# Layer 0's input projection loaded by rows in four pieces instead of by column slices, and its latent part accumulated piece by piece

## The reference, cut to what matters

```python
def conv_mla_mixer(x, cos, sin, w_in, b_in, conv_w, conv_b, ...):
    h = x @ w_in + b_in                      # (256, 1024) @ (1024, 1440)
    conv_in = h[..., :1024]                  # value | gate of the convolution, 4 chunks of 128 channels each
    q_lat, kv_lat, k_rope = h[..., 1024:1280], h[..., 1280:1408], h[..., 1408:]   # "latent" part, 416 columns
    ...
    u = a * jax.nn.sigmoid(g)                # then depthwise conv of width 31 (conv_w: 31 x 512)
    q  = rms_norm(q_lat, q_norm_g) @ w_uq
    kv = rms_norm(kv_lat, kv_norm_g) @ w_ukv
    o = causal_block_attention(q, k, v, ...)
    return jnp.concatenate([u, o], axis=-1) @ w_out + b_out
```

## Time and profile before

| | |
|---|---|
| device time, median of 3 runs | 1470.88 us (1467.9 to 1471.5) |
| span of the profiled execution, first to last instruction | 1469.8 us |
| time of the profiled execution beside its span | not listed apart from the span |
| PE busy | 1402.9 us, 95% of the span |
| DVE, ACT, POOL busy | 38%, 26%, 5% |
| DMA | 447.33 MB, mean 304 GB/s |
| chain that ended last | PE 90%, DVE 4%, issue 3%, ACT 1%, DMA 1% |

### The profile page before, as it was taken

One profiled execution on the slowest core, in us unless ns is written; L12 is line 12 of the kernel. 1 busy time (PEld: TensorE's weight loads), 2 busy tenths in 40 slices (PEclk: granted clock), 3 DMA queues, 4 the chain that ended last, 5 costly groups with the idle time before them and its releaser, 6 DMA issues.

```text
span 1469.8 us, 19916 instructions
## 1 busy us (share of the span) xinstructions
PE 1402.9 (95%) x7220; PEld 727.8 (50%) x7220; DVE 564.8 (38%) x1147; ACT 388.1 (26%) x857; POOL 76.7 (5%) x100
## 2 busy tenths in 40 slices
PE   6988999999999999999699999999999999999996
PEld 4764744444444444444288857444444444444441
DVE  2593534333333333433422235333333333333324
ACT  2561222222222222222122222222222222222221
POOL 2251100000000000000140000000000000000000
PEclk9999999999999999999899999999999999999998
DMA  9223679989999999998831415699889999999980
GB/s 338 83 115 143 235 286 381 379 346 378 381 382 381 381 379 381 380 377 345 278 137 58 163 38 230 279 381 381 358 361 382 380 380 383 380 382 380 381 360 30
DMA packets 80326, 447.33 MB, mean 304 GB/s; under 512 B 7437, under 2 KB 25289, under 8 KB 30616
## 3 DMA queue, kind: packets, MB, share of 16 engines
q1 hardware_dynamic: 77264, 439.25, 74.1%
q0 software_dynamic: 1904, 6.46, 1.3%
q10 hardware_dynamic: 1112, 1.01, 0.2%
HBM read 445.61 MB, written 1.05 MB: 304 GB/s over the span
## 4 chain that ended last, share of the span: by engine, by line
PE 90%; DVE 4%; issue 3%; ACT 1%; DMA 1%; DVEq 0%; POOLq 0%; POOL 0%; SPq 0%; ACTq 0%
PE bank L910 30%; PE bank L932 16%; PE bank L884 12%; PE bank L978 10%; PE bank L769 4%; PE bank L733 4%; PE bank L646 2%; PE bank L772 2%; PE bank L920 2%; PE bank L837 2%; DVE mixT L1635 2%; DMA ring<-in_l_w_in 1%; PE bank L947 1%; PE bank L875 1%; PE bank L628 1%
## 5 line engine op out<-in xcount | busy, mean ns | idle before, releaser
L910 PE MATMUL bank<-ring,big 128*64 128x512 f32 x2048 | 446.5, 594 | 0.0
L910 PEld LDWEIGHTS bank<-ring,big 128*64 128x64 f32 x2048 | 144.7, 137 | 279.1 <-issue 279.1
L932 PE MATMUL bank<-ring,big 128*64 128x512 f32 x1024 | 233.8, 598 | 2.2 <-ACT big L1193 2.2
L978 PE MATMUL bank<-big 128*128 128x512 bf16 x768 | 182.1, 385 | 9.4 <-DVE big L1607 5.3
L884 PE MATMUL bank<-att,side 128*128 128x256 bf16 x1536 | 187.6, 276 | 0.0
L884 PEld LDWEIGHTS bank<-att,side 128*128 128x128 bf16 x1536 | 169.4, 146 | 29.3 <-issue 25.4
L1592 DVE TENSOR_TENSOR big<-big,bank 128x256 f32<-128x256 f32 x64 | 27.0, 421 | 377.3 <-ACT big L1189 377.3
L1600 DVE SCALAR_TENSOR_TENSOR V<-bank,gcol,big 128x512 f32<-128x512 f32 x128 | 96.1, 750 | 148.1 <-ACT big L1199 148.1
L1189 ACT ACTIVATE big<-bank 128x256 f32<-128x256 f32 x64 | 24.6, 384 | 405.5 <-PE bank L910 405.5
L1199 ACT ACTIVATE big<-bank,gcol 128x512 bf16<-128x512 f32 x128 | 87.9, 687 | 156.6 <-PE bank L932 156.6
L932 PEld LDWEIGHTS bank<-ring,big 128*64 128x64 f32 x1024 | 67.8, 136 | 122.5 <-issue 119.6
(11 more groups left out here) (236 smaller groups left out, 1007.0 us busy)
## 6 DMA issues: line engine op xcount, KB each, us to landing
ring<-in_l_exp_w_gate SPq DMA_DIRECT2D x128, 1024.0 KB, 8.7
ring<-in_l_exp_w_up SPq DMA_DIRECT2D x128, 1024.0 KB, 10.7
ring<-in_l_exp_w_down SPq DMA_DIRECT2D x128, 1024.0 KB, 14.0
ring<-in_l_w_in SPq DMA_DIRECT2D x16, 1024.0 KB, 12.4
ring<-in_l_w_out SPq DMA_DIRECT2D x8, 1024.0 KB, 8.9
par<-in_l_ln_g POOLq DMA_DIRECT2D x4, 512.0 KB, 9.2
par<-in_l_ln_b POOLq DMA_DIRECT2D x4, 512.0 KB, 11.5
ring<-in_l_sh_w_gate SPq DMA_DIRECT2D x2, 1024.0 KB, 5.8
```

What stands on the lines that cost most here:

```text
L910: ins = mm(ps[SLOTS * q:SLOTS * q + SLOTS, :], xg[:, c, SLOTS * j:SLOTS * j + SLOTS], both[:, c], start=(c == 0), stop=(c == C - 1))
L932: ins = mm(ps[SLOTS * q:SLOTS * q + SLOTS, :], hidT[pr][:, m, SLOTS * q:SLOTS * q + SLOTS], wt[:, m, HALF * h:HALF * h + HALF], start=(m = ...
L978: ins = mm(ps[:], hot[:, pr, P * tb:P * tb + P], ys[k][:, pr, HALF * h:HALF * h + HALF], start=(pr + k == 0), stop=(pr == 1 and k == 2))
```

## The change

The 1440 columns of `l0_w_in` are one contiguous run for each of the eight chunks c that a partition holds (row 8p + c of the matrix). The changed kernel loads two chunks at a time: four pieces of 1.47 MB, in each of which a partition's bytes are one run of 11,520 bytes. `win0`, 8 x 1440 floats for each partition, covers ring units 0 to 5.

```diff
+L0IN = 2 * CONV + LAT
+WPIECES = 4
+WCHUNKS = C // WPIECES
+WPIECE = WCHUNKS * L0IN
...
-    for k in range(4):
+    for k in range(WPIECES):
         u.add(("in0", k), k)
-    u.add(("lat", 0), 4)
     u.add("uq", 6)
     u.add("ukv", 7)
     for k in range(4):
-        u.add(("out0", k), 8 + k)
+        u.add(("out0", k), (0, 1, 10, 11)[k])
     for k in range(3):
-        u.add(("shared", 0, k), k)
-    first = {0: 1, 1: 0}
+        u.add(("shared", 0, k), 3 + k)
+    first = {0: 2, 1: 1}
...
-        diag = ring[:, 4 * UNIT:4 * UNIT + TAPS * P].rearrange("p (k n) -> p k n", k=TAPS)
+        diag = ring[:, 8 * UNIT:8 * UNIT + TAPS * P].rearrange("p (k n) -> p k n", k=TAPS)
+        win0 = ring[:, 0:C * L0IN].rearrange("p (c n) -> p c n", c=C)
...
-            win = I["l0_w_in"].rearrange("(p c) n -> p c n", c=C)
-            wl = ring[:, 4 * UNIT:4 * UNIT + C * LAT].rearrange("p (c n) -> p c n", c=C)
-            load(("lat", 0), wl, win[:, :, 2 * CONV:])
-            for k in (0, 2):
-                load(("in0", k), by_chunk(unit(("in0", k))), win[:, :, 256 * k:256 * k + 256])
+            win = I["l0_w_in"].rearrange("(p c) n -> p (c n)", c=C)
+            for k in range(WPIECES):
+                cs = slice(WPIECE * k, WPIECE * k + WPIECE)
+                load(("in0", k), ring[:, cs], win[:, cs])
...
-            for k in (1, 3):
-                load(("in0", k), by_chunk(unit(("in0", k))), win[:, :, 256 * k:256 * k + 256])
...
-                for k in range(4):
+                for k in range(4) if L else (2, 3, 0, 1):
                     load((f"out{L}", k), by_pair(unit((f"out{L}", k))), wout[k],
-                         after=("qk", k) if L else None)
+                         after=("qk", k) if L else ("ag", 3) if k < 2 else None)
...
-                    held = [("ag", 3), "convT", "convT", ("q", 1, 1), ("kv", 1, 1), mix,
-                            mix, mix, mix, sgu, sgu, sdn]
+                    held = [("q", 1, 1), ("kv", 1, 1), "convT", "convT", mix, mix,
+                            mix, mix, ("ag", 3), sgu, sgu, sdn]
+                    early = (0, 1, 8, 2, 3, 4, 5, 6, 7, 9, 10, 11)
...
-            unit_wait(pe, ("lat", 0))
-            for tb in range(TB):
-                ps = bank_open(pe, ("lat", tb))
-                for c in range(C):
-                    ins = mm(ps[:, 0:LAT], xT[:, c, P * tb:P * tb + P], wl[:, c, :], start=(c == 0), stop=(c == C - 1))
-                bank_made(ins, ("lat", tb))
...
+            for k in range(WPIECES):
+                unit_wait(pe, ("in0", k))
+                for tb in range(TB):
+                    ps = bank_open(pe, ("lat", tb)) if k == 0 else bank[banks.at[("lat", tb)][0]]
+                    for c in range(WCHUNKS * k, WCHUNKS * k + WCHUNKS):
+                        ins = mm(ps[:, 0:LAT], xT[:, c, P * tb:P * tb + P], win0[:, c, 2 * CONV:],
+                                 start=(c == 0), stop=(c == C - 1))
+                    if k == WPIECES - 1:
+                        bank_made(ins, ("lat", tb))
+                if k == 0:
+                    columns()
...
-            bank_read(act, ("lat", 1))
             diagonals(0, EARLY)
```

More of the change, by code:

```diff
@@ L185, in plan_units @@
     for k in range(4):
-        u.add(("out0", k), 8 + k)
+        u.add(("out0", k), (0, 1, 10, 11)[k])
     for k in range(3):
-        u.add(("shared", 0, k), k)
-    first = {0: 1, 1: 0}
+        u.add(("shared", 0, k), 3 + k)
+    first = {0: 2, 1: 1}
     u.loop(0, [((j, k), 3 * ((first[0] + j) % 4) + k) for j in range(GE) for k in range(3)], NGRP)
     for k in range(12):
-        u.add(("in1", k), (3 + k) % 12)
+        u.add(("in1", k), (6 + k) % 12)
     for k in range(4):
-        u.add(("out1", k), 3 + k)
+        u.add(("out1", k), 6 + k)
     for k in range(3):
-        u.add(("shared", 1, k), 9 + k)
+        u.add(("shared", 1, k), k)
     u.loop(1, [((j, k), 3 * ((first[1] + j) % 4) + k) for j in range(GE) for k in range(3)], NGRP)
@@ L505, in prog_sync @@
                 if L == 0:
-                    held = [("ag", 3), "convT", "convT", ("q", 1, 1), ("kv", 1, 1), mix,
-                            mix, mix, mix, sgu, sgu, sdn]
+                    held = [("q", 1, 1), ("kv", 1, 1), "convT", "convT", mix, mix,
+                            mix, mix, ("ag", 3), sgu, sgu, sdn]
+                    early = (0, 1, 8, 2, 3, 4, 5, 6, 7, 9, 10, 11)
                 else:
                     held = [("v", 1), ("v", 2), ("v", 3)] + [mix] * 4 + [("qk", 4), ("qk", 5), sgu, sgu, sdn]
[L510 to L514, removed]
+                    early = range(3 * GE)
+                for j, w in (divmod(k, 3) for k in early):
+                    bank_read(sp, held[3 * j + w])
+                    sp.dma_start(loop_weights(L, j, w), expert_weights(L, j, w))\
+                      .then_inc(S(f"unit_full{loop_unit(L, j, w)[0]}"), 16)
                 lp = ExpertLoop(L, banks, S, bank)
@@ L621, in prog_tensor, with columns @@
                 xt_there(0, tb)
-            wl = ring[:, 4 * UNIT:4 * UNIT + C * LAT].rearrange("p (c n) -> p c n", c=C)
-            unit_wait(pe, ("lat", 0))
-            for tb in range(TB):
-                ps = bank_open(pe, ("lat", tb))
-                for c in range(C):
-                    ins = mm(ps[:, 0:LAT], xT[:, c, P * tb:P * tb + P], wl[:, c, :], start=(c == 0), stop=(c == C - 1))
-                bank_made(ins, ("lat", tb))
-            pe.wait_ge(S("rows0"), 48)
-            ps = bank_open(pe, "cols0")
-            flip(ps[:, 0:12], rows0, ident[0:12, 0:12])
-            for j in range(CC):
-                ins = flip(ps[:, 12 + TAPS * j:12 + TAPS * j + TAPS], taps0[:, P * j:P * j + P], ident[0:TAPS, 0:TAPS])
-            bank_made(ins, "cols0")
+            def columns():
+                pe.wait_ge(S("rows0"), 48)
+                ps = bank_open(pe, "cols0")
+                flip(ps[:, 0:12], rows0, ident[0:12, 0:12])
+                for j in range(CC):
+                    ins = flip(ps[:, 12 + TAPS * j:12 + TAPS * j + TAPS], taps0[:, P * j:P * j + P],
+                               ident[0:TAPS, 0:TAPS])
+                bank_made(ins, "cols0")
+            for k in range(WPIECES):
[9 more added lines that the diff above has]
+                    columns()
             def value_gate(j):
@@ L642, in value_gate @@
                 for s in range(2):
-                    w = by_chunk(unit(("in0", 2 * s + j // 2)))
-                    unit_wait(pe, ("in0", 2 * s + j // 2))
                     for c in range(C):
-                        ins = mm(ps[:, T * s:T * s + T], w[:, c, P * (j % 2):P * (j % 2) + P], xT[:, c, :],
+                        ins = mm(ps[:, T * s:T * s + T], win0[:, c, CONV * s + P * j:CONV * s + P * j + P], xT[:, c, :],
                                  start=(c == 0), stop=(c == C - 1))
```

## The result

| kernel | median, us | runs | lowest to highest | profiled execution: time, span |
|---|---|---|---|---|
| before | 1470.88 | 13 | 1467.9 to 1471.59 | span 1469.8 |
| changed | 1473.19 | 13 | 1469.87 to 1475.86 | 1475.86, span 1474.0 |

The ratio of the changed kernel to the one before is 1.0019, 95% interval 1.0011 to 1.0027: 1.6 to 4.0 us slower, a real loss but inside the 0.3% that I called no change. (The ratio is close to that of the means; the medians differ by 2.3 us.) The median lies 3.1 us under the forecast of 1476.3. The profiled execution is the slowest of the 13; its span minus that of before, 4.2 us, is above what the ratio gives (2.8).

The account below looks back on a forecast made before the run. It took a chain of waits up to the q product's end to bound the kernel, everything later passing the delay on. 8.9 - 1.7 - 1.8 = +5.4 us gave 1476.3 us, range 1468 to 1480.

Parts of the forecast that it names:

- The mechanism: At kernel start: SP's long packets alternate with ACT's small ones, so PE stands at late `rows0` before 12 latent matmuls.
- Rivals A: At the early loads: the turns are no obstacle, `rows0` lands by 18 us; 1462.5 us, chance 0.16.
- rival B: At the early loads: 11.52 KB runs go as two packets, `rows0` lands at 22.6; 1470.6 us, chance 0.17.
- Term 1: At the early loads: when the pieces and `rows0` land; `rows0` at 28.3 us, between 27.2 and 29.9.
- Term 2: From `rows0` to `value_gate(0)`: 11.1 us, mostly twelve latent matmuls; `value_gate(0)` starts at 39.4, +8.9 us.
- Term 3: Hole ahead of the q product: early diagonals on ACT shorten it from 2.88 to 1.15 us, -1.7.
- Term 4: In the q product: without the long hole the clock does not fall; 5.3 us and not 7.09, -1.8.
- Handed on whole: From the q product to the kernel's end: a lead or delay at the q product's end passes on in full.
- the terms that I put at nothing: After the q product: expert loops, later `par` loads, eight loads at `value_gate(3)` and diagonals moved to unit 8 cost nothing.
- C: The forecast itself: slower, 1476.3 us, with its own range of 1473.5 to 1480; chance 0.67.

Follow-up runs that it names:

- run 9: The changed kernel measured and profiled once more with no edit: 1472.9 us, ratio 1.0024 to the kernel before.
- run 1: Changed kernel with the wait for the small rows and the column transposes moved from behind the first piece to behind the fourth: 1466.63 us, ratio 0.9965.
- run 2: Changed kernel with the 31 tap rows loaded by two DMAs of 16 and 15 rows, same queue and order: 1465.96 us, ratio 0.9955.
- run 4: Changed kernel with each piece made of chunks k and k+4, two runs of 5,760 bytes a partition instead of one of 11,520: 1467.5 us, ratio 0.9974.
- run 7: Changed kernel with taps split into 16 and 15 rows and the four small loads ahead of the `lpar` loads in ACT's queue: 1462.74 us, ratio 0.9946.
- run 8: The kernel before, measured and profiled once more with no edit: 1470.85 us, ratio 1.0005.
- run 5: Changed kernel with ACT's diagonals waiting for the latent product again, and 27 of them early instead of 20: 1478.43 us, ratio 1.0056.
- run 3: Kernel before with the tap rows loaded by two DMAs of 16 and 15 rows: 1468.37 us, ratio 0.9984.
- run 6: Kernel before, short packets kept, with the wait for the small rows and the column transposes moved ahead of the latent product: 1467.23 us, ratio 0.9972.
- run 10: Kernel before with column slices, taps split, small loads first in ACT's queue and column transposes ahead of the latent product: 1462.28 us, ratio 0.9957.

## Why the prediction came out as it did

All by its own steps; times in us.

| | forecast | changed | again (run 9) |
|---|---|---|---|
| `rows0` landed | 28.3 | 27.25 | 27.39 |
| `value_gate(0)` starts | 39.4 | 38.51 | 39.30 |
| end of `value_gate(0)` to q product | 1.15 | 1.0 | 1.0 |
| q product | 5.3 | 5.40 | 5.40 |
| q end, against before's 47.54 | +5.4 | +4.3 | +5.1 |

**The mechanism was right.** PE did 8 records, stood until 27.3 with the wait ended by the taps' load, and had 24 records behind it. Runs 1, 2 and 4 each take one link of that chain away (the place of the wait, the one engine, the packet size) and win back 5.7 to 7.2 us of the changed kernel's 1473.19; run 7 takes the place in the queue away on top of run 2's link, and wins back 10.4. Rivals A and B are excluded as accounts of the change itself: the turns are an obstacle, and 11.52 KB is one packet.

**Term 1 was 1.05 too large.** The transfer behind x was 20.2 us by the count (6.2 to 26.4), and I stretched it for mixed queues to at most 22.9. (The prediction's words have the 22.9 stretched once more; its bounds, 27.2 and 29.9, are the right ones of the sum.) With long packets the engines ran at 420 GB/s (13 to 16 us), so the unstretched figure, 27.2, was the right end of my bounds; the last `lpar` load, forecast through at 16.3, landed at 16.4. That is partly luck: run 2 shows closing packets of 4 bytes that the count of turns left out, each a turn. The count was good for this kernel to 1 us and for the split taps only to 3.

**Term 2**: 11.3 from `rows0` to `value_gate(0)`, forecast 11.1; 11.9 in run 9. It rested on slow records under a granted clock that read 1.00. In the changed kernel the clock accounts for them (line 641 by windows, columns as in the earlier trace rows):

```profile
28.00:31.80 3.80, 3.80 (x6) 2.02 (x7) 0.50 0.94 375
31.80:38.50 6.70, 6.70 (x19) 3.33 (x18) 1.00 0.04 15
```

and so it does in run 8, the second profile of before (line 628):

```profile
16.70:22.80 6.10, 6.01 (x9) 3.19 (x10) 0.50 1.07 375
22.80:31.20 8.40, 8.39 (x24) 4.19 (x23) 1.00 1.08 366
```

Records of 0.63 to 0.67 us on average stand at 0.50 (1.2 GHz), records of 0.35 at 1.00 (2.4 GHz). The first profile of before has no record of the clock earlier than 20.5 us, where its slow records end; the 1.00 of the earlier trace rows for 16.70 to 20.40 stands for no record, and is no reading of the clock.

**Term 3**: -1.9, forecast -1.7; run 5 puts ACT back and the hole is 2.79, seven added diagonals included. DVE's normalisation stayed under its cover as said (43.3 against `value_gate(0)`'s end at 45.4). 0.19 us came from `value_gate(0)` itself (6.91 after 7.10), which I had not priced. Together 8.04 - 0.19 - 1.89 - 1.69 = +4.27 at the q product's end.

**Term 4 was the step with the wrong basis.** It took the clock's fall in the q product as a property of the kernel before, tied to its hole. Of the four profiles with a hole of 2.2 us, two have the fall (before, run 1: 7.09) and two not (runs 3 and 8: 5.40); with 2.79 us (run 5) it is there; with 0.34 to 0.75 us, in seven profiles, never. So no short hole was followed by it, but a short hole is worth 1.7 us only against those executions of before that have the fall. Against run 8 the changed kernel is 4.8 us later at that point and run 9 5.6.

**Handed on whole: it was, but for falls of the clock farther on.** At q end the changed kernel is 4.3 (run 9: 5.1) us behind the first profile of before; the medians leave 2.3 and the ratios 1.0019 and 1.0024, 2.8 and 3.5 us. From the q product on, PE's program is the same before and after, so the delay can be read instruction by instruction. It is 4.0 to 4.4 us from 54 to 162 us: the terms that I put at nothing were nothing there. Then it jumps to 7.6 within the router's products and the shared expert's behind them, stays at 7.4 to 7.9 through the first expert loop and the second attention layer, falls back to 4.4 at the same products of layer 1, and is 4.2 at the end.

These products are the same work each time, L853 and L837 before, L861 and L845 after. PE's timeline of the first profile of before:

```profile
161.76 3.75 PE L853 MATMUL bank<-rw,xT 128*128 128x64 f32 x32 [0.83 <-ACT xT L1019]
...
895.10 4.63 PE L853 MATMUL bank<-rw,xT 128*128 128x64 f32 x32 [0.83 <-ACT xT L1019]
899.53 9.79 PE L837 MATMUL bank<-xT,ring 128*128 128x128 f32 x64
```

and of the changed kernel:

```profile
166.13 5.03 PE L861 MATMUL bank<-rw,xT 128*128 128x64 f32 x32 [0.83 <-ACT xT L1027]
170.95 9.39 PE L845 MATMUL bank<-xT,ring 128*128 128x128 f32 x64
...
902.74 3.76 PE L861 MATMUL bank<-rw,xT 128*128 128x64 f32 x32 [0.83 <-ACT xT L1027]
```

The shared expert's products take 7.36 us where they don't follow such a fall. In the changed kernel the granted clock was 0.74 from 165 to 172 us where before had 1.00 from 161 to 173: a mean between the levels 2.4 and 1.2 GHz. Before has it at 0.57 from 897 to 905, where the changed kernel has 1.00 from 902 to 914.

A third such place, A, is layer 0's `w_out` product (0.51 from 116 to 123 us in before, 1.00 from 115 to 128 in run 9). With B for the router and shared expert of layer 0 and C for those of layer 1, a fall costs 3.0 us at A and 3.3 at B or C. (Falls near 90, 720 and 1455 us are in every profile.) The profiles differ in which they have (differences in us to before, whose q end is 47.54, whose profile has a span of 1469.8 and falls at A and C; medians to the one beside each):

| | changed | 1 | 2 | 3 | 4 | 5 | 6 | 7 | 8 | 9 | 10 |
|---|---|---|---|---|---|---|---|---|---|---|---|
| q end | +4.3 | -2.6 | -1.7 | -3.1 | -1.0 | +7.7 | -2.8 | -8.4 | -0.6 | +5.1 | -6.9 |
| falls | A, B | A, B | A, B | A, C | B | A, C | none | B | A, C | none | A |
| span | +4.2 | -3.0 | -2.1 | -3.2 | -4.4 | +6.9 | -9.2 | -11.8 | -1.0 | -1.2 | -10.4 |
| median | +2.3 | -4.7 | -5.3 | -2.9 | -3.8 | +7.5 | -3.7 | -8.2 | 0.0 | +2.3 | -8.3 |

In all eleven the span follows from q end and the falls, to 0.5 us (run 5: 0.8). In run 9, for instance, 5.05 - 3.0 - 3.3 = -1.25, and its span gives -1.2. So the lead or delay at the q product's end goes through the whole kernel.

The changed kernel's single runs spread over 6.0 us, those of before over 3.7: the profile with two falls is the slowest of its 13 (1475.86) and run 9's with none is near the fastest of its ten (1470.49). The 2.3 us between the medians can then be the whole delay with one fall fewer in the middle run than before has, which would give 1.0 to 2.1. That is an estimate and not shown: runs without a profile list only a mean clock (0.981 in the run of 1475.86, 0.986 in that of 1469.87). What decides where the clock falls stays open, and a forecast of the median should have carried a spread for it.

**Chances.** I had 0.51 on slower by over 0.3% and 0.33 on the case within it, which came, by the forecast's own mechanism and not by rival B: 5.4 was too near the bound of 4.4 for that split, once 1 us of term 1 and the falls of the clock are counted. The median lies in the range of 1468 to 1480, but just under C's own, 1473.5 to 1480.

## What to carry to other kernels

In these runs two DMA queues that share engines alternate packet by packet (121 to 123, with 1.21 and 0.05 MB), so making one queue's runs longer takes bandwidth from every small load beside it: count the turns of what is waited for before lengthening a stream, put the small loads that an engine waits for first in their queue, and cut them so that they spread over the engines (31 rows on one engine cost 2.3 us of landing even beside short packets). Then ask again what the long runs are worth: here the taps split, the small loads first and the columns transposed early brought 8 us, with long runs (run 7) or with short ones (run 10). And one profile is one execution: before a gain or loss at one point is compared with a median, count the falls of the clock behind it. A wait that is moved ahead is priced by what is queued behind it, at the time when its data comes in the new kernel and not in the old.

## What the runs showed of the hardware that was not expected

- The alternation holds down to records of 4 bytes: 255 packets with 2.57 MB against 256 with 0.19 MB in 7 us (run 2), 113 of the 511 under 512 bytes.
- With packets of 11.52 KB in the stream the 16 engines moved 420 GB/s (13 to 16 us), beside 413 with 5.76 KB (run 4) and 419 with 8 KB; in these rows nothing above 8 KB was left to win.
- The latent product's first records cost a different time in each profile: the 8 of the first piece took 4.70 to 5.88 us in six profiles of kernels that have it, and before's 32 took 13.28 and 14.40. Where the trace has the clock, the slow records end with its stretch at 0.50 (Term 2).
- A fall of the clock in the middle of the kernel costs 3.0 to 3.3 us, and which of three places have one differs between executions of one kernel: the changed kernel's two profiles have two falls and none.
